# Compressed convolution of an attention block with the chunks as the stationary operand and two positions' weights moving

## The reference

```python
CMP_LEN, CMP_STRIDE = 32, 16
def compress_kv(kv, pos, w1, b1, w2):        # kv [1, 512, 4, 128]
    n_cmp = (S - CMP_LEN) // CMP_STRIDE + 1  # 31 windows
    idx = jnp.arange(n_cmp)[:, None] * CMP_STRIDE + jnp.arange(CMP_LEN)[None, :]
    blocks = kv[:, idx] + pos[None, None, :, None, :]
    blocks = jnp.transpose(blocks, (0, 1, 3, 2, 4)).reshape(B, n_cmp, G, CMP_LEN * dh)
    hdn = jax.nn.gelu(blocks @ w1 + b1)      # w1 [32 * 128, 128]
    return hdn @ w2
```

## Time and profile before

| | us |
|---|---|
| median of 3 runs | 2169.27 (2169.15 to 2170.48) |
| the profiled execution | 2169.41 |
| its span | 2167.6 |
| TensorE busy | 2156.6 (99%) |
| VectorE busy | 1550.5 (72%) |
| ScalarE busy | 1036.9 (48%) |

### The profile page before, as it was taken

How to read it: one execution, slowest core, us unless ns; L and a number is a source line. 1 busy time by engine, 2 the same in 40 slices (tenths; PEclk the granted TensorE clock), 3 DMA queues, 4 the chain that set the end, 5 groups by cost and what they waited for, 6 DMA issues and landing times.

```text
span 2167.6 us, 29862 instructions
## 1 busy us (share of the span) xinstructions
PE 2156.6 (99%) x11261; PEld 1850.3 (85%) x11261; DVE 1550.5 (72%) x2230; ACT 1036.9 (48%) x1481; POOL 103.9 (5%) x123
## 2 busy tenths in 40 slices
PE   9999999999999999999999999999999999999999
PEld 8898988989889998788888888888888888888887
DVE  6333566675676554897777777777777898989898
ACT  5332344443453344854445445444544565555553
POOL 1001000000000000000000000000000000000000
PEclk9999999999999999999999999999999999999999
DMA  5444232232224223655555455465555677666655
GB/s 179 116 111 99 82 68 60 69 69 59 53 75 147 78 69 107 199 157 174 141 156 188 113 171 174 129 176 164 161 157 162 199 211 234 185 199 194 180 143 163
DMA packets 209871, 301.94 MB, mean 139 GB/s; under 512 B 18924, under 2 KB 116497, under 8 KB 208321
## 3 DMA queue, kind: packets, MB, share of 16 engines
q1 hardware_dynamic: 197618, 254.74, 37.4%
q0 software_dynamic: 12112, 45.31, 9.9%
HBM read 236.79 MB, written 28.59 MB: 122 GB/s over the span
## 4 chain that ended last, share of the span: by engine, by line
PE 96%; DVE 2%; ACT 1%; issue 1%; DMA 0%; POOL 0%; SPq 0%; DVEq 0%; ACTq 0%
PE ps L1736 93%; PE ps L2048 1%; PE ps L2118 1%; DVE wl L1088 1%; ACT wh L674 0%; DMA x_rows<-in_x_dram 0%; DVE x_rows L1121 0%; ACT left_val L934 0%; DVE hTl L1088 0%; PE ps L2028 0%; PE ps L2083 0%; DVE ptl L1409 0%; ACT sq L969 0%; DVE pbuf L1386 0%; ACT pbuf L834 0%
## 5 line engine op out<-in xcount | busy, mean ns | idle before, releaser
L674 ACT ACTIVATE wh<-g 128x1024 fp32r<-128x1024 f32 x462 | 490.1, 1062 | 580.4 <-PE ps L1736 444.0
L1088 DVE TENSOR_TENSOR wl<-g,wh 128x1024 fp32r<-128x1024 f32 x462 | 565.1, 1224 | 227.3 <-PE ps L1736 219.6
L1736 PE MATMUL ps<-wh,left_hi 128*128 128x512 f32 x1232 | 481.9, 391 | 0.9 <-DVE wl L1088 0.5
L1736 PE MATMUL ps<-wh,left_lo 128*128 128x512 f32 x1232 | 479.7, 389 | 0.0
L1736 PE MATMUL ps<-wl,left_hi 128*128 128x512 f32 x1232 | 479.4, 389 | 0.0
L1736 PEld LDWEIGHTS ps<-wh,left_hi 128*128 128x128 f32 x1232 | 231.3, 188 | 50.4 <-issue 2.6
L1736 PEld LDWEIGHTS ps<-wh,left_lo 128*128 128x128 f32 x1232 | 231.2, 188 | 48.4
L1736 PEld LDWEIGHTS ps<-wl,left_hi 128*128 128x128 f32 x1232 | 231.3, 188 | 47.2
L1736 PE MATMUL ps<-wh,down_hi 128*128 128x512 f32 x616 | 239.8, 389 | 0.0
L1736 PE MATMUL ps<-wh,down_lo 128*128 128x512 f32 x616 | 239.7, 389 | 0.0
L1736 PE MATMUL ps<-wl,down_hi 128*128 128x512 f32 x616 | 239.6, 389 | 0.0
(11 more groups left out here) (212 smaller groups left out, 3027.9 us busy)
## 6 DMA issues: line engine op xcount, KB each, us to landing
g<-in_ffn_w_gate_dram SPq DMA_DIRECT2D x176, 256.0 KB, 3.2
g<-in_ffn_w_up_dram SPq DMA_DIRECT2D x176, 256.0 KB, 4.2
g<-in_ffn_w_down_dram SPq DMA_DIRECT2D x176, 256.0 KB, 5.1
raw<-in_nsa_w_in_dram SPq DMA_DIRECT2D x152, 256.0 KB, 3.1
g<-g POOLq DMA_DIRECT2D x66, 512.0 KB, 5.0
down_val<-m_scratch SPq DMA_DIRECT2D x77, 256.0 KB, 4.8
raw<-in_nsa_w_out_dram SPq DMA_DIRECT2D x64, 256.0 KB, 3.1
m_scratch<-work SPq DMA_DIRECT2D x22, 384.0 KB, 2.9
```

What stands on the lines that cost most here:

```text
L674: return nc.scalar.activation(dst, src, ACT.Copy)
L1088: nc.vector.tensor_tensor(dst, src, hi.bitcast(f32), ALU.subtract).then_inc(done, 1)
L1736: return nc.tensor.matmul(out_, a, b, start=start, stop=stop, skip_group_check=True)
```

## The change

1. `conv_unit`: the chunks are stationary (`cbh` or `cbl`, one position o of all 32 chunks x 4 groups, 128 columns), and the weights of position o for e = 0 and e = 1 move side by side (256 columns). A stage has 48 products of 256 columns instead of 96 of 128. The bank holds, for each chunk and group, two partial results.
2. The weights are laid out for that: a unit holds positions o = 4j to 4j + 3 for both e. It is still loaded by two transfers of 256 KB with pieces of 512 bytes.
3. The sum over the halves: ScalarE copies the bank to `z_sb` (128 x 256) after it has split unit n + 4 at the last conv unit. After the next unit (13 or 25) TensorE runs `shift_add`: two fp32 products with the identity, one shifted by 4 columns, which also turn the result back, and one fp32 product that sums `bias_sum` over partitions.
4. The position terms: VectorE multiplies the raw weights of each conv unit with the position terms, 1024 columns, ahead of the unit's low half (`bias_product`), and sums the 8 positions of each output column behind it (`bias_add`). After the fourth unit it sums the four partial results. The reads of both sums step over 128 columns (512 bytes) from one element to the next.
5. `hb`, the gelu and the key chain move one unit later, and the gaps in the key chain are closed, so that it ends one unit earlier. The copies of the position terms into `cbh` and `cbl` go.

```diff
-K_CONV0, KC0, V_CONV0 = 9, 13, 21
+K_CONV0, KC0, V_CONV0 = 9, 14, 21
...
-        w1_v = cmp_w1[0].rearrange("t (j l p) c -> t j p l c", l=8, p=P)
+        w1_v = cmp_w1[0].rearrange("t (e j o p) c -> t e j p o c", e=2, o=4, p=P)
...
-                    unit(n, k_halves(n, w1_v[ty, j], 8))
+                    dst = raw[:, n % RAW, :].rearrange("p (o e c) -> p o e c", o=4, e=2)
+                    unit(n, [(dst[:, :, e, :], w1_v[ty, e, j]) for e in range(2)])
...
                 if kind == "conv" and j == 3:
-                    act.wait_ge(hb_ready, ty + 1)
...
+                    act.wait_ge(units_used, n + 1)
+                    copy(z_sb[:, :, :].rearrange("p e c -> p (e c)"), bank(4)[:, 0:2 * P]).then_inc(z_copied, 1)
+                if n == K_CONV0 + 4:
+                    gelu(0)
...
             def split(n, per=0, i=0):
                 wait(dve, hi_ready, n + 1, per, i)
                 width = unit_width(n)
+                if unit_kind(n)[0] == "conv" and n < P0:
+                    bias_product(n)
                 lo(wl[:, n % RING, 0:width], raw[:, n % RAW, 0:width], wh[:, n % RING, 0:width], lo_ready)
+                if unit_kind(n)[0] == "conv" and n < P0:
+                    bias_add(n)
+
+            def bias_product(n):
+                _, ty, j = unit_kind(n)
+                weights = raw[:, n % RAW, :].rearrange("p (o e c) -> p o e c", o=4, e=2)
+                pos = cols[:, ty * CMP_LEN:(ty + 1) * CMP_LEN].rearrange("p (e q o) -> p q o e", e=2, o=4)[:, j, :, :]
+                pos = pos.rearrange("p o (e a) -> p o e a", a=1).to_broadcast([P, 4, 2, P])
+                own.done(nc.vector.tensor_tensor(w1_pos[:, :, :, :], weights, pos, ALU.mult))
+
+            def bias_add(n):
+                _, ty, j = unit_kind(n)
+                own.settle()
+                own.done(nc.vector.reduce_sum(bias_part[:, j, :], w1_pos[:, :, :, :].rearrange("p o e c -> p c (o e)"), axis=AX.X))
+                own.settle()
+                if j == 3:
+                    if ty:
+                        dve.wait_ge(shift_done, ty)
+                    nc.vector.reduce_sum(bias_sum[:, :], bias_part[:, :, :].rearrange("p j c -> p c j"), axis=AX.X)\
+                        .then_inc(bias_ready, 1)
...
+                if n == K_CONV0 + 4:
+                    hidden_bias(0)
...
-                for ll in range(8):
-                    l = 8 * j + ll
-                    o, e = l % CMP_STRIDE, l // CMP_STRIDE
-                    at = slice(ll * P, (ll + 1) * P)
-
-                    w, win = P, slice(2 * e, 2 * e + S // CMP_STRIDE)
-                    last = mm3(bank(4)[:, e * GROUPS:e * GROUPS + w], (wh[:, n % RING, at], wl[:, n % RING, at]),
-                               (cbh[:, o, win, :].rearrange("p c g -> p (c g)"),
-                                cbl[:, o, win, :].rearrange("p c g -> p (c g)")), l == 0, l == CMP_LEN - 1)
+                for oo in range(4):
+                    o, at = 4 * j + oo, slice(oo * 2 * P, (oo + 1) * 2 * P)
+                    last = mm3(bank(4)[:, 0:2 * P],
+                               (cbh[:, o, 1:-1, :].rearrange("p c g -> p (c g)"),
+                                cbl[:, o, 1:-1, :].rearrange("p c g -> p (c g)")),
+                               (wh[:, n % RING, at], wl[:, n % RING, at]), o == 0, o == CMP_STRIDE - 1)
                 last.then_inc(units_used, 1)
+
+            def shift_add(ty):
+
+                pe.wait_ge(z_copied, ty + 1)
+                pe.wait_ge(bias_ready, ty + 1)
+                if ty:
+                    pe.wait_ge(gelu_done, 1)
+                mm(bank(5)[:, 0:NC4], z_sb[:, 0, :], ident[:, 0:NC4], start=True)
+                mm(bank(5)[:, 0:NC4], z_sb[:, 1, :], ident[:, GROUPS:GROUPS + NC4], stop=True)
+                mm(bank(5)[:, P:P + 1], bias_sum[:, :], inv128[:, 0:1], True, True).then_inc(shift_done, 1)
...
+                if n in (K_CONV0 + 4, V_CONV0 + 4):
+                    shift_add(int(n > V_CONV0))
```

More of the change, by code:

```diff
@@ L227, in nsa_swiglu_block @@
         cbh, cbl = over("cbh", CB, q_at, f32r), over("cbl", CB, q_at + 4 * CB[1] * CB[2] * CB[3], f32r)
+        z_sb = over("z_sb", [P, 2, P], x_at)
+        w1_pos = over("w1_pos", [P, 4, 2, P], x_at + 4 * 1024)
+        bias_part, bias_sum = over("bias_part", [P, 4, P], x_at + 8 * 1024), over("bias_sum", [P, P], x_at + 10 * 1024)
         stage_at = nc.sbuf_base
@@ L741, in project_compressed @@
                     square(sq[:, 0, 0:NC4], bank(6)[:, 0:NC4]).then_inc(kc_sq, 1)
-                if n == KC0 + 6:
+                if n == KC0 + 4:
                     act.wait_ge(kc_norm, 1)
@@ L746, in project_compressed, with gelu @@
                 if kind == "conv" and j == 3:
-                    act.wait_ge(hb_ready, ty + 1)
[L748 to L756, removed]
+                    act.wait_ge(units_used, n + 1)
+                    copy(z_sb[:, :, :].rearrange("p e c -> p (e c)"), bank(4)[:, 0:2 * P]).then_inc(z_copied, 1)
+                if n == K_CONV0 + 4:
+                    gelu(0)
+            def gelu(ty):
+                act.wait_ge(hb_ready, ty + 1)
+                src = bank(5)[:, 0:NC4]
+                if ty == 0:
+                    dsts = [hdn[:, :, :].rearrange("p c g -> p (c g)")]
+                else:
+                    src = src.rearrange("p (c g) -> p g c", g=GROUPS)
+                    dsts = [hdn3[:, :, r, 0:N_CMP] for r in range(3)]
+                for dst in dsts:
+                    last = nc.scalar.activation(dst, src, ACT.Gelu_apprx_tanh, bias=hb[:, ty:ty + 1])
+                last.then_inc(gelu_done, 1)
             for n in range(V_CONV0 + 4):
@@ L810, in _ @@
                 split(n + RING)
+                if n == V_CONV0 + 4:
+                    gelu(1)
                 if n == P0 + 1:
@@ L1164, in project_compressed @@
                     own.done(nc.vector.tensor_scalar(gains[:, :], cols[:, 67:70], cols[:, 66:67], None, ALU.mult))
[L1165 to L1173, removed]
                 if kind == "columns" and j in (3, 7):
@@ L1183, in project_compressed @@
                         .then_inc(kc_raw, 1)
-                if n == KC0 + 2:
+                if n == KC0 + 1:
                     dve.wait_ge(kcsum_done, 1)
@@ L1187, in project_compressed @@
                         .then_inc(kc_den, 1)
-                if n == KC0 + 3:
+                if n == KC0 + 2:
                     dve.wait_ge(kc_root, 1)
@@ L1191, in project_compressed @@
                         .then_inc(kc_diag, 1)
-                if n == KC0 + 5:
+                if n == KC0 + 3:
                     dve.wait_ge(kcb_done, 1)
@@ L1196, in project_compressed @@
                         .then_inc(kc_norm, 1)
-                if n == KC0 + 7:
+                if n == KC0 + 5:
                     dve.wait_ge(kc_hi, 1)
@@ L1200, in project_compressed, with hidden_bias @@
                        kch[:, :, 0:N_CMP], kc_lo)
[L1201 to L1207, removed]
+                if n == K_CONV0 + 4:
+                    hidden_bias(0)
+            def hidden_bias(ty):
+                dve.wait_ge(shift_done, ty + 1)
+                own.done(nc.vector.tensor_scalar(hb[:, ty:ty + 1], bank(5)[:, P:P + 1], float(P), None, ALU.mult))
+                own.settle()
+                nc.vector.tensor_tensor(hb[:, ty:ty + 1], hb[:, ty:ty + 1], cols[:, 64 + ty:65 + ty], ALU.add)\
+                    .then_inc(hb_ready, 1)
             for n in range(V_CONV0 + 4):
@@ L1253, in _ @@
                 split(n + RING)
+                if n == V_CONV0 + 4:
+                    hidden_bias(1)
                 if n == P0 + 1:
@@ L1881, in _ @@
                        True, True).then_inc(kc_done, 1)
-                if n == KC0 + 2:
+                if n == KC0 + 1:
                     pe.wait_ge(kc_sq, 1)
                     mm(bank(7)[0:NC4, 0:1], sq[:, 0, 0:NC4], inv128[:, 0:1], True, True).then_inc(kcsum_done, 1)
-                if n == KC0 + 4:
+                if n == KC0 + 3:
                     pe.wait_ge(kc_diag, 1)
```

9 lines of the change are left out of this document (5 added, 4 removed).

## The result

| | before | after |
|---|---|---|
| median, us | 2169.39 (2168.71 to 2170.48, 20 runs) | 2173.87 (2171.43 to 2176.56, 20 runs) |
| ratio to before | 1 | 1.002 (95%: 1.0013 to 1.0027) |
| profiled execution, us | 2169.41 (span 2167.6) | 2172.03 (span 2170.3) |

The account below looks back on a forecast made before the run. TensorE, busy 99% at full clock, was taken as the bound. Products gain 9.8 us; `shift_add` costs 1.4, low-half waits 3.5 + 4.1, copy waits 1.9 + 1.5: with rounding 2.7 us longer, 2172.1 us, range 2167.0 to 2175.8.

Parts of the forecast that it names:

- Conv products: TensorE's convolutions: 48 products of 256 columns at 0.120 us, 5.76 us per stage instead of 10.66; 9.8 us saved in all.
- `shift_add`: Three small fp32 products on TensorE at 0.23 us each: 0.7 us more per stage, 1.4 in all.
- Price of VectorE's work: VectorE per conv unit: product 1.23 us, strided sum 2.0, low half 1.23, together 4.46; last sum 1.1.
- rival (a): VectorE's sums cost the neighbouring-element price, 3.7 us per unit: 0 to +1 us, about 2169.9 us; chance 0.22.
- First wait: TensorE waits for VectorE's low halves up to units 13 and 25: 3.5 us at the keys, 4.1 at the values.
- Second wait: TensorE waits ahead of `shift_add` for ScalarE's bank copy behind unit 16's (28's) split: 1.9 us at keys, 1.5 at values.
- the copy of the bank comes before TensorE asks for it: Sign of being wrong, ahead of the identity products: a TensorE wait of about 1.5 to 2 us for ScalarE was expected there.
- The clock: TensorE's granted clock in the changed profile: expected at full in every slice, with no time for it in the sum.
- rival (d): TensorE's clock halves after a 3.5 us stall; one unit at half speed costs 5.5 us: 2177.6 us; chance 0.06.
- The sum without the clock: All terms, both stages: stages lose 1.2 us (keys) and 1.5 us (values), 2.7 us longer, 2172.1 us.
- Rival (b): VectorE's extra is hidden, only the bank copy waits: 2.0 and 1.8 us won, 2165.6 us; chance 0.06.
- The gelu: ScalarE's gelu needs about 3 us after `shift_add` and follows during unit 14's 5.5 us on TensorE.

Follow-up runs that it names:

- packed sum: Changed kernel with the product written at a 32-byte step so that the sum reads neighbouring elements: 2175.08 us, ratio 1.0025.
- filler: Changed kernel with 20 transposes of the identity on TensorE behind the last conv unit, ahead of the wait for units 13 and 25: 2170.32 us, ratio 1.0007.
- early copy: Changed kernel with ScalarE's copy of the bank ahead of its split of unit 16 (and 28) instead of behind it: 2170.73 us, ratio 1.0009.
- both edits: Changed kernel with early copy and late sums at once: 2169.46 us, ratio 1.0002.
- short queues: Changed kernel with a tree of neighbouring adds, last two sums later, bank copy ahead of unit 15's split, hb and gelu ahead of 17's: 2162.66 us, ratio 0.9969.
- no position work: Changed kernel without VectorE's product and sums, `bias_sum` set to zero once: 2167.64 us, ratio 0.9991.
- late sums: Changed kernel with the last two conv units' sums and the last sum behind the low halves of units 13 and 14 (25, 26): 2170.67 us, ratio 1.0005.
- the changed kernel again: Changed kernel as it is, timed again on the same chip as other kernels of that call: 2172.60 us, ratio 1.0019.

## Why the prediction was right, and where it was not

The range held the time, and the forecast's side, slower, came out. The 4.5 us measured lie a hair beyond the 4.3 us that the prediction had set as the edge of "within". That lies on the side to which it gave 0.28 and not 0.69, though the measured interval (0.13% to 0.27%) covers the edge. But the closeness of 2172.1 to the profiled 2172.03 is partly luck: two errors cancelled. Without the clock the stages were put too dear, and the clock was put at nothing.

- **Conv products**: 0.12 us spacing, as forecast: the four units took 81.99 - 73.17 less the waits of 2.42 and 0.32, 6.1 us with the slower restarts behind them, for 5.76 forecast.
- **`shift_add`**: 0.7 us forecast, 0.69 measured (90.42 to 91.11).
- **Price of VectorE's work**: right. The sum was taken at 2.0 and measured 1.98 to 2.03, the last one at 1.1 and measured 1.02. The row of `kcl` in the earlier trace rows carried it, although its step is 16 bytes and that of the sums 512, and rival (a) fell; the packed sum showed both sides of the stride.
- **First wait**: right in cause. Unit 13 was put at 82.4 and started at 81.99. The term was 0.4 too large, mostly because instructions that don't wait for the one ahead overlap it by 0.09 us. TensorE's waits for low halves were 0.32 + 2.42 us at the keys and 1.01 + 2.29 at the values, for 3.5 and 4.1 forecast. Leaving the work out removed them.
- **Second wait**: right in cause at the keys, and the copy's end at 89.8 was measured at 90.36. But the wait was 1.19 us for 1.9, since unit 13 ran slower, and at the values there was none for 1.5: the copy ended at 145.93, as unit 25, at half the clock, was ending. One of the prediction's signs of being wrong was that "the copy of the bank comes before TensorE asks for it". There it was met, by the clock and not by an early copy. That the wait adds to what follows was only partly true: moving the copy uncovered the gelu.
- **The clock**: the step that failed. The row of the page shows no dip, but only because its slices are 54 us long; windows of 2 us do show it. It was rival (d), with a chance of 0.06, at the price of a whole unit at half speed, 5.5 us, from a stall of 3.5 us. It happened after stalls of 2.4 and 2.3 us, in both stages of the first trace and in one of the second, and lasted about 3 us each time, which costs half of that, about 1.6 us a stage, where nothing covers it. In the profiled execution the slower unit 13 merely filled the wait for the copy. Over all executions the filler's gain is the nearest thing to a price: with it the changed kernel takes 2170.3 instead of 2172.6 to 2173.9. Rival (d) belonged into the forecast, as a term of up to 2 or 3 us, and not as a chance of 0.06.
- **The sum without the clock** was thus too pessimistic by 1.5 to 1.8 us: 2.7 us over the kernel before were forecast, and with the filler 1.2 were measured (2170.3 us, where 2172.1 was forecast). In that run's trace the stages lose 0.4 and 0.7 us by TensorE's timeline, measured from the start of each convolution to units 14 and 26, not 1.2 and 1.5 as forecast. The overlap of VectorE's instructions, and unit 16's split starting 3.9 us after the low half of 14 rather than 4.4, are what the trace shows for it. In the first trace of the changed kernel that step took 5.06 us and the key stage lost 1.77, so this term varies between executions.
- **Rival (b)**: 2165.6 was worked out for VectorE's work hidden, and 2165.48 measured with that work left out, once the clock was kept up.
- **The gelu** behind the split of unit 16 or 17: I wrote that it needs about 3 us and is covered. In the changed kernel that is so. With the early copy, with both edits and with the position work in the old kernel it is the next wait (0.56 to 2.03 us at the keys); without the position work and with short queues it is not.

## What to carry to other kernels

Before adding work to an engine that is half idle, look at what it does just ahead of the instruction that the bound engine and the loads wait for. Here VectorE got 7.5 us of work between `cbl` and the low half of the next unit; leaving the position work out made the changed kernel 5.0 to 6.2 us faster. With the wait for the copy, `shift_add` and the clock it cost more than the 9.8 us of saved products gave. When a wait is removed from a chain of rings, the next one in the queue order shows up, so work out all queues behind the same load before expecting the sum. And on TensorE a stall can have a second price behind it: put something harmless there, or count about 3 us after it at half the clock.

## What was not expected of the hardware

- The granted clock went to half (0.50 in a 2 us window, products spaced 0.43 us instead of 0.23) after TensorE had stood still for 2.3 to 2.4 us in an otherwise full stretch, for about 3 us. The length of the wait does not decide alone. The clock also fell after 1.61 us (no position work, values), 2.06 and 2.90 (late sums), and 2.48 (packed sum, keys, 0.54 at 94 to 96 us), but stayed at 1.00 after 2.34 (no position work, keys), 2.41 (the changed kernel again, keys), 2.37 and 2.29 (early copy) and 2.03 (both edits). What else decides is open. The Trainium skill ("TensorE: Matmul & The Clock Gate", Why this matters for your kernels) names a length of idle gap to stay below. The traces do not agree: gaps that the clock fell after here were shorter than that, and the measurement decides.
- 18 to 20 useless transposes in such a gap made the kernels 2.2 us (no position work) and 2.3 to 3.5 us (changed kernel) faster. In the kernel before with the position work 14 of them changed nothing that stands clear of the noise (2173.74 to 2172.82 us).
- On VectorE, fp32 operands with a step of 512 bytes (read) or 32 bytes (written) cost 1.98 and 2.13 us for 1024 elements, against 1.20 to 1.22 for neighbours. The Trainium skill ("SBUF — State Buffer", Specifications) gives the rule, that section without a price; the trace agrees with it.
